# Two matmuls for the high part, then two for the low part, or high and low in turn: the order inside one weight unit

## The reference, cut to what matters

```
proj   = h @ w_in                          # 2048 x 11344
y      = y_a @ w_a, y_b @ w_b, merged @ w_o
ffn    = (silu(a) * b) @ w_down            # a, b from a short convolution of h @ w_up
second = conformer convolution (two products, depthwise taps), squared-relu MLP (two products)
```

## Time and profile before

| | |
|---|---|
| median of 3 runs | 2752.69 us |
| lowest, highest | 2751.36, 2753.84 us |
| the profiled execution: time | 2752.69 us |
| its span, first to last instruction | 2750.9 us |
| mean granted clock of TensorE | 0.979 of full speed |
| TensorE matmuls busy | 2629.0 us, 96% |
| TensorE weight loads busy | 2289.5 us, 83% |
| VectorE busy | 1938.8 us, 70% |
| ScalarE busy | 1209.3 us, 44% |

### The profile page before, as it was taken

How to read it: one execution, slowest core, us unless ns; L and a number is a source line. 1 busy time by engine, 2 the same in 40 slices (tenths; PEclk the granted TensorE clock), 3 DMA queues, 4 the chain that set the end, 5 groups by cost and what they waited for, 6 DMA issues and landing times.

```text
span 2750.9 us, 39657 instructions
## 1 busy us (share of the span) xinstructions
PE 2629.0 (96%) x14749; PEld 2289.5 (83%) x14749; DVE 1938.8 (70%) x2742; ACT 1209.3 (44%) x1559; POOL 101.5 (4%) x145
## 2 busy tenths in 40 slices
PE   3499999999998999999999999998999999999998
PEld 2488888888887888888888888886888888888886
DVE  6977778886887888855666537997676654566544
ACT  1244654444654655544555541004454433444443
POOL 0011111100001000000000000000000000000000
PEclk8599999999999999999999999999999999999999
DMA  8798777865776777755666544551556555666553
GB/s 324 290 302 260 222 242 241 251 199 161 226 252 226 238 247 248 229 190 186 189 190 187 181 138 147 153 153 64 191 181 187 188 190 190 186 189 190 184 184 107
DMA packets 492579, 557.32 MB, mean 203 GB/s; under 512 B 18854, under 2 KB 458279, under 8 KB 492199
## 3 DMA queue, kind: packets, MB, share of 16 engines
q1 hardware_dynamic: 474023, 488.50, 55.9%
q0 software_dynamic: 18432, 67.12, 8.1%
HBM read 553.45 MB, written 2.10 MB: 202 GB/s over the span
## 4 chain that ended last, share of the span: by engine, by line
PE 92%; DVE 4%; issue 1%; DMA 1%; SPq 1%; ACT 1%; DVEq 0%; POOL 0%; ACTq 0%
PE ps L1383 52%; PE ps L1385 26%; PE ps L1656 8%; PE ms L1414 2%; DVE wlo L820 1%; DVE norm_rows L901 1%; PE ms L1423 1%; DMA att<-in_w_ada 1%; PE ms L1681 1%; DMA att<-in_x 0%; DVE tCDE L901 0%; PE ms L1514 0%; SPq L380 0%; DVE norm_rows L843 0%; PE ms L1666 0%
## 5 line engine op out<-in xcount | busy, mean ns | idle before, releaser
L820 DVE TENSOR_TENSOR wlo<-raw,whi 128x1024 fp32r<-128x1024 f32 x794 | 971.3, 1225 | 658.2 <-ACT whi L505 649.0
L1383 PE MATMUL ps<-xhl,whi 128*128 128x512 f32 x4352 | 1383.2, 399 | 23.1 <-DVE xhl L865 16.7
L505 ACT CAST whi<-raw 128x1024 fp32r<-128x1024 f32 x794 | 831.2, 1050 | 1159.7 <-PE ps L1385 1079.8
L1385 PEld LDWEIGHTS ps<-xhl,wlo 128*128 128x128 f32 x4352 | 820.4, 189 | 194.2
L1385 PE MATMUL ps<-xhl,wlo 128*128 128x256 f32 x4352 | 857.8, 279 | 0.0
L1383 PEld LDWEIGHTS ps<-xhl,whi 128*128 128x128 f32 x4352 | 667.4, 189 | 33.6 <-issue 32.7
L1383 PE MATMUL ps<-ghl,whi 128*128 128x512 f32 x1024 | 320.0, 394 | 0.0
L1385 PEld LDWEIGHTS ps<-ghl,wlo 128*128 128x128 f32 x1024 | 192.2, 188 | 44.5
L1656 PE MATMUL ps<-xg,raw 128*128 128x256 f32 x1024 | 221.3, 379 | 0.0
L1383 PE MATMUL ps<-fhl,whi 128*128 128x512 f32 x704 | 220.4, 394 | 0.0
L1656 PEld LDWEIGHTS ps<-xg,raw 128*128 128x128 f32 x1024 | 194.6, 190 | 26.5
(11 more groups left out here) (225 smaller groups left out, 1535.0 us busy)
## 6 DMA issues: line engine op xcount, KB each, us to landing
raw<-in_w_in SPq DMA_DIRECT2D x176, 512.0 KB, 4.4
raw<-in_w_up SPq DMA_DIRECT2D x176, 512.0 KB, 3.8
ada<-in_w_ada POOLq DMA_DIRECT2D x128, 512.0 KB, 4.6
raw<-in_ffn_w_up SPq DMA_DIRECT2D x128, 512.0 KB, 3.7
raw<-in_ffn_w_down SPq DMA_DIRECT2D x128, 512.0 KB, 3.3
raw<-in_conv_w_pw SPq DMA_DIRECT2D x96, 512.0 KB, 3.6
raw<-in_w_down SPq DMA_DIRECT2D x88, 512.0 KB, 3.3
att<-in_w_ada SPq DMA_DIRECT2D x32, 1024.0 KB, 7.2
```

The costliest lines, as they stand in the source:

```text
L505: nc.scalar.copy(whi[t % SPL][:, :, :], raw[t % RAW][:, :, :]).then_inc(s_hi, 1)
L820: nc.vector.tensor_tensor(wlo[t % SPL][:, :, :], raw[t % RAW][:, :, :], whi[t % SPL][:, :, :].bitcast(F32), ALU.subtract).then_inc(s_lo, 1)
L1383: mm(o[:, m, :, :], whi[t % SPL][:, c, m * P:(m + 1) * P], x, start=first and c == 0, stop=last and c == KC - 1, skip_group_check=True)
L1385: ins = mm(o[:, m, 0, :], wlo[t % SPL][:, c, m * P:(m + 1) * P], x[:, 0, :], start=False, stop=last and c == KC - 1, skip_group_check=True)
```

## The change

Inside `unit`, the two loops over m (first all high matmuls, then all low ones) become one, whose body is the existing `products`: high and low of m = 0, then high and low of m = 1. The `start` and `stop` flags of each matmul are the same as before, and the unit's last matmul is still the low one of m = 1.

```diff
                 for c in range(KC):
                     x = rhs(c)
                     for m in range(PC):
-                        mm(o[:, m, :, :], whi[t % SPL][:, c, m * P:(m + 1) * P], x, start=first and c == 0, stop=last and c == KC - 1, skip_group_check=True)
-                    for m in range(PC):
-                        ins = mm(o[:, m, 0, :], wlo[t % SPL][:, c, m * P:(m + 1) * P], x[:, 0, :], start=False, stop=last and c == KC - 1, skip_group_check=True)
+                        w = slice(m * P, (m + 1) * P)
+                        ins = products(o[:, m, :, :], whi[t % SPL][:, c, w], wlo[t % SPL][:, c, w], x, first and c == 0, last and c == KC - 1)
                 ins.then_inc(s_used, 1)
```

## The result

The changed kernel took 2769.45 us (median of 4 runs, 2768.43 to 2771.26), the kernel before 2753.26 us on the same chip (2751.36 to 2753.84). The ratio is 1.006, 95% interval 1.0043 to 1.0079: 16 us slower, where no change was forecast. The profiled execution of the changed kernel took 2764.23 us with a span of 2762.4 us, 11.5 us more than that of before.

The account below looks back on a forecast made before the run. TensorE was taken as the bound, with 3168 chunks of 0.6965 us making 2207 us, 80% of the span. Nothing removed or added, 3168 x 0 = 0 us, so 2752.7 us was forecast, range 2745 to 2761 us.

Parts of the forecast that it names:

- The count of work: In `unit`: same four loads and four matmuls per chunk, no wait or DMA added, removed or moved; other engines' cost 0.
- Point 1: Weight loads in `unit`: two under long and two under short matmuls per chunk in both orders; cost 0 ns.
- Point 2: Staying in one PSUM bank: small columns in `products` already show this order, 0.6957 to 0.6973 us per two pairs; cost 0.
- Point 3: Long and short matmuls alternating in `unit`: 0.698 us per chunk, at most +1 to +2 ns, +3 to +7 us.
- Rival A: Same-bank stall of each low matmul behind its high one: +4 ns per chunk, +13 us, 2765 us; chance 0.10.
- Rival B: Bank changes cost time now, so the new order is faster: 2664 us, or 2743 us in small form; chance 0.06.
- the missing 56 ns per chunk: Gap between a chunk's 0.640 us at one column per cycle and the measured 0.696 us, perhaps four bank changes of 14 ns.

Follow-up runs that it names:

- run 3: Changed order, with 80 instead of 128 columns per weight block outside each group's first chunk (other 48 output rows left out): 2733.18 us, one run.
- run 4: Old order, with 80 columns per weight block outside each group's first chunk (other 48 output rows left out): 2756.62 us, one run.
- run 5: Changed order, with the low matmuls taking both halves of the input, so all four matmuls have 512 columns: 3436.69 us.
- run 6: Old order, with the low matmuls taking both halves of the input, so all four matmuls have 512 columns: 3437.90 us.
- run 7: Changed order, with three small tiles allocated ahead of xhl, which lies 2944 bytes higher: 2771.14 us against 2754.29 us for the kernel before, ratio 1.0065.
- run 9: Old order, with three small tiles allocated ahead of xhl, which lies 2944 bytes higher: 2754.53 us against 2753.24 us, ratio 1.0008.
- run 10: Old order, with 64 unused bytes ahead of xhl, moving it and all behind it: 2738.82 us, one run.
- run 11: Old order, with 192 unused bytes ahead of xhl, moving it and all behind it: 2740.51 us, one run.
- run 12: Old order, every input tile 64 bytes past a multiple of 512 against the weights: 2738.01 us against 2752.71 us, ratio 0.9941.
- run 13: Changed order, every input tile 64 bytes past a multiple of 512 against the weights: 2777.43 us, ratio 1.0089.
- run 14: Old order, with xhl 128 and fhl, ghl, att_r 96 bytes past a multiple of 512 against the weights: 2764.76 us, one run.
- run 15: Old order, with 64 unused bytes ahead of whi, so inputs and both weight tiles move together: 2752.55 us, one run.
- run 16: Old order, with 64 unused bytes between whi and wlo, so wlo and the inputs move and whi stays: 2768.66 us, one run.
- run 1: Old order with the low matmuls swapped (high 0, high 1, low 1, low 0): 2753.64 us against 2753.54 us, ratio 0.9998.
- run 8: Changed order, with a one-column matmul ahead of each group of the later stages: 2777.26 us, one run.

## Why the prediction was wrong

The count of work held: no instruction, wait or transfer was added or moved, the other engines' busy times stayed, TensorE stayed the bound, so what the units gained in length is in the time. Points by their numbers in the prediction:

- *Point 1, the weight loads: the step that failed.* "Two and two, cost 0 ns" took the price of a load under a matmul to depend only on how long the matmul is. Runs 3 to 7 and 9 to 16 show that the price of the stream depends on the width of the weight blocks (with their output) and on the places of the load's and the matmul's tiles against each other, and that the stream as a whole settles in a pattern. A count of pairs can't price that. The step also took a load with a low matmul behind it and one with a high matmul behind it to cost the same, from rows of 0.01 us; by the starts in the trace of before, a low matmul is followed after 116.4 ns by a low and after 118.4 ns by a high one on `ghl`. The mean chunk went from 697.5 to 702.4 ns by the spacings under 300 ns, +4.9 ns where 0 was forecast, and 3168 x 4.9 ns = 15.5 us; the sum of the units grew by 14.7 us, the median of the runs by 16 us.
- *Point 2, the small columns.* They showed the new order at 348.2 ns a pair, and I noted the 80 columns as the one difference, then set it aside, because staying in a bank was the only thing I asked of them. For the bank the answer was right: run 1 pays nothing for it. For the order it was misleading: with 80 columns almost throughout, the new order is the quicker one (run 3).
- *Point 3, spacings of unlike matmuls.* It gave +1 to +2 ns per chunk as the upper bound, with the right sign and too small. To read the spacings finer would not have saved it: on `ghl` before, high to low takes 234.5 ns and low to high 118.4 ns, which makes 705.8 ns for a chunk in the new order, and 702.0 ns came, with spacings of 230.5 and 120.4 ns. They belong to the pattern, not to the pair.
- *Rival A* had the side, the place of the loss and, with +4 ns per chunk, nearly its size, but the wrong mechanism, and I gave it 0.10. *Rival B* was wrong about banks (run 1 changes them half as often and gains nothing), but right that the missing 56 ns per chunk are not a fixed cost: moving tiles by 64 bytes gives 7 of them back.

**What is shown, and what is not.** Shown: the price of an order depends on the place of inputs against weights (runs 7, 9 to 16), on the width of the weight blocks, with that of the output (3, 4), and on there being short matmuls (5, 6); for the same tiles the new order has two patterns, chosen in its long stages by how a stage is entered (after, run 8). Not shown is why a place has the patterns that it has. That the load's read and the matmul's read get in each other's way in SBUF is what these have in common, but no view shows the read itself, so it stays an inference. By the patterns, the changed kernel could have come out anywhere from 2752 us (all `xhl` units at 2773 ns) to 2777 us (all at 2827 ns), other things equal, which is an estimate: 456 x -13.5 or +40 ns, and 235 x 22 ns for the rest, on top of 2753 us. Where in between it came out was luck to the forecast; no row of before shows that the new order has two patterns.

The Trainium skill, "TensorE: Matmul & The Clock Gate", section "Step-by-step: what each phase is for", says that TensorE has separate read ports for the moving operand and for the weight load, and that loading the next weights doesn't steal read bandwidth from the running matmul. The runs here don't fit that: with identical instructions, a move of the input by 64 bytes against the weight tiles changes a unit from 2787 to 2760 ns, and a move of both together leaves it at 2787 ns. They show the time and not the ports.

## What to carry to other kernels

In a kernel of dense matmuls, each with a load of its own, the order of the matmuls and the start addresses of the input tiles against the weight tiles were worth some tenths of a per cent to one per cent here, and couldn't be priced from the spacings of another order, width or place. Measure them, and measure them together. Trying a few pads of 64 bytes is cheap, and here gave more (0.6%) than any order did. Before trusting a small difference, look whether the units of one loop have the same length throughout: if they come in two lengths, the time of the kernel depends on how its stages happen to be entered.

## What the runs showed of the hardware

- A stream of loads and matmuls falls into exactly repeating patterns. The undisturbed units of a stage repeat one length, to 1 ns, or a cycle of two or three (2760; 2773; 2787; 2793; 2799 and 2821; 2830, 2831 and 2819), a unit being four chunks. The order of the matmuls and the places of inputs and weights against each other decide which of them occur, and in the two long stages of the changed kernel and run 8 the entry decided between two.
- The same matmuls of 512 columns, with loads of 128 columns, take 226.7 or 233.3 ns each on `xhl` and on `ghl`, inputs at different places (runs 5, 6), with the granted clock at 1.00. Plain fp32 records of 256 columns take 215.8 ns, whatever the bank.
- A matmul that adds to the addresses that the one ahead of it has just written cost nothing measurable in run 1 (ratio 0.9998, interval 0.9989 to 1.0008).
- At a granted clock of 0.50 a chunk took 1.28 us, at 1.00 it took 0.696 us (kernel before).
